# Differential attention: the score products of the two maps issued in turns, behind one wait for both exponentials

## The chip, the cores and the metric

The kernel runs on 1 core of a Trainium2 chip. The metric is the time of one execution in device microseconds (us). The kernel before takes 4272.95 us (median of 3 runs, 4268.02 to 4278.03).

## The reference

One step of a two-layer backbone for 512 latent tokens and 128 context tokens. The change lies in layer 0, which mixes tokens by differential attention with 8 heads. Each head has two score maps c = 0, 1, each from 64 rows of query and key:

```
s = einsum('bqhd,bkhd->bhqk', qblk, k) * scale      # q, k: 2 * 8 maps of width 64
p = softmax(s)                                      # per map
w = p[:, :, 0] - lam * p[:, :, 1]                   # one weight map per head
o = einsum('bhqk,bkhd->bqhd', w, v)                 # v: width 128 per head
```

Latent queries read 512 latent keys and 128 cached context keys in one softmax. The 128 context queries read only their own 128 keys. After the attention come a norm, an output product, and PEER expert retrieval; layer 1 uses another attention (MLA) and PEER again.

## The kernel before

The program is a row of blocks, with a barrier of all engines at the end of each: modulation and norms, q/k/v products (`diff_qkv`), `diff_attention` (lines 439 to 569), a norm (`diff_subnorm`), the output product (`out_product`), the experts, then the same for layer 1. The change touches only `scores(w)` in `diff_attention`.

`diff_attention` works through 40 items, 8 heads times 5 query blocks of 128 queries. Blocks 0 to 3 of a head are latent (640 keys), block 4 is context (128 keys). The order of each engine is written out by hand, and the engines are tied by semaphores:

- TensorE (PE), in iteration w: the scores of item w (lines 455 to 465), the product with V of item w-3 (`values`, line 484), the transposes of item w-2 (`turns`, line 474). The scores of map c go to PSUM banks 2c and 2c+1: 512 columns in the first, 128 in the second (lines 461, 462), or 128 columns alone for a context item (line 464). The operands are float32, and each such product appears in the trace as two weight loads (PEld) and two matmuls. Map 0 reads partitions 0 to 63 of q and k, map 1 partitions 64 to 127.
- VectorE (DVE): `maxima(w+1)`, then `weights(w)`. `maxima` waits for the scores of map 0 (`da_s` at 2w+1), takes the row maximum (line 515) and scales it (517), then does the same for map 1 (`da_s` at 2w+2). `weights` turns the two exponentials into one weight map (523 to 529).
- ScalarE (ACT): the two exponentials of item w (`exps`, line 547), each behind its scaled maximum; then the copy of the transposes of item w-2 (556) and of the result of item w-3 (561).

There is one set of score banks. So the scores of map c of item w wait until the exponential of the same map of item w-1 has read its banks: `da_exp` at 2(w-1)+c+1 in line 459. The semaphore goes up once per exponential, at the end of its ACTIVATION_READ_ACCUMULATOR.

Of the kernel before, what the change touches and what calls it, by code (L numbers as in the profile page):

```python
# [25 lines left out]
P = 128  # L26
D = 1024
DC = D // P
TS, TP, TC = 512, 128, 128
T = TS + TP  # L30
TK = T + TC
# [28 lines left out]
def mixed(nc, cst, inp, outs, g_dram, x_dram):  # L60
# [3 lines left out]
    def sem(name):  # L64
        if name not in sems:
            sems[name] = es.enter_context(nc.semaphore(name))
        return sems[name]

    def sb(stack, name, shape, dt=F32):
        return stack.enter_context(nc.sbuf_tensor(name, shape, dt))  # L70
# [18 lines left out]
    ps = es.enter_context(nc.psum_tensor("ps", [P, 8, 512], F32))  # L89
# [3 lines left out]
    def bank2(b, n=T, p=P):  # L93

        return ps[0:p, b:b + 2, :].rearrange("p a n -> p (a n)")[:, 0:n]
# [343 lines left out]
    def diff_attention(qT, kT, V, rsq, oT, pr, pT):  # L439

        items = [(hd, qb) for hd in range(HDA) for qb in range(TB)]

        def width(qb):
            return T if qb < 4 else TP

        with nc.Block() as block:
            @block.sync
            def _(sp):
                sp.wait_ge(sem("stored"), 32)

            @block.tensor
            def _(pe):
                def scores(w):
                    hd, qb = items[w]
                    for c in range(2):
                        q = qT[64 * c:64 * c + 64, hd, qb * P:(qb + 1) * P]
                        k = kT[64 * c:64 * c + 64, hd, :]
                        if w:
                            pe.wait_ge(sem("da_exp"), 2 * (w - 1) + c + 1)
                        if qb < 4:  # L460
                            pe.matmul(ps[:, 2 * c, :], q, k[:, 0:TS], start=True, stop=True)
                            mm = pe.matmul(ps[:, 2 * c + 1, 0:TC], q, k[:, T:TK], start=True, stop=True)
                        else:
                            mm = pe.matmul(ps[:, 2 * c, 0:TP], q, k[:, TS:T], start=True, stop=True)
                        mm.then_inc(sem("da_s"), 1)

                def turns(w):
                    hd, qb = items[w]
                    blocks = (0, 1, 2, 3, 5) if qb < 4 else (4,)
                    pe.wait_ge(sem("da_w"), 8 * (w + 1) + (4 if w + 1 < len(items) else 0))  # L470
                    if w >= 1:
                        pe.wait_ge(sem("da_pT"), w)
                    for k in range(len(blocks)):
                        mm = pe.transpose(bank2(4)[:, k * P:(k + 1) * P], pr[:, w % 3, 0, k * P:(k + 1) * P], ident)
                    mm.then_inc(sem("da_t"), 1)

                def values(w):
                    hd, qb = items[w]
                    blocks = (0, 1, 2, 3, 5) if qb < 4 else (4,)
                    pe.wait_ge(sem("da_pT"), w + 1)  # L480
                    if w >= 2:
                        pe.wait_ge(sem("da_o"), w - 1)
                    for k, kb in enumerate(blocks):
                        mm = pe.matmul(ps[:, 6 + w % 2, 0:P], V[:, kb, hd * P:(hd + 1) * P], pT[:, w % 2, k * P:(k + 1) * P],
                                       start=k == 0, stop=k == len(blocks) - 1)
                    mm.then_inc(sem("da_pv"), 1)

                for w in range(len(items) + 3):
                    if w < len(items):
                        scores(w)  # L490
                    if w >= 3:
                        values(w - 3)
                    if 2 <= w < len(items) + 2:
                        turns(w - 2)

            @block.vector
            def _(v):
                s = sem("da_w")
                M = len(items)

                def z_(w):
                    return small[:, 16 * (w % 2):16 * (w % 2) + 16]

                def at(w, k):

                    if k <= 4:
                        return k if w == 0 else 8 * w - 4 + k
                    return 8 * w + k + (4 if w + 1 < M else 0)

                def maxima(w):  # L510
                    hd, qb = items[w]
                    n, z = width(qb), z_(w)
                    for c in range(2):
                        v.wait_ge(sem("da_s"), 2 * w + c + 1)
                        v.tensor_reduce(z[:, c:c + 1], bank2(2 * c, n), AX, ALU.max).then_inc(s, 1)
                        v.wait_ge(s, at(w, 2 * c + 1))
                        v.tensor_scalar(z[:, 2 + c:3 + c], z[:, c:c + 1], rsq[:, 1, qb, 2 * hd + c:2 * hd + c + 1],
                                        None, ALU.mult).then_inc(s, 1)

                def weights(w):  # L520
                    n, z = width(items[w][1]), z_(w)
                    v.wait_ge(sem("da_exp"), 2 * w + 2)
                    v.reciprocal(z[:, 6:8], z[:, 4:6]).then_inc(s, 1)
                    v.wait_ge(s, at(w, 5))
                    v.tensor_tensor(z[:, 8:9], z[:, 7:8], lam[:, 4:5], ALU.mult).then_inc(s, 1)
                    p0, p1 = pr[:, w % 3, 0, 0:n], pr[:, w % 3, 1, 0:n]
                    v.tensor_scalar(p0, p0, z[:, 6:7], None, ALU.mult).then_inc(s, 1)
                    v.wait_ge(s, at(w, 7))
                    v.scalar_tensor_tensor(p0, p1, z[:, 8:9], p0, ALU.mult, ALU.add).then_inc(s, 1)

                maxima(0)
                for w in range(M):
                    if w + 1 < M:
                        maxima(w + 1)
                    weights(w)

            @block.scalar
            def _(act):
                def exps(w):
                    hd, qb = items[w]  # L540
                    n = width(qb)
                    z = small[:, 16 * (w % 2):16 * (w % 2) + 16]
                    if w >= 3:
                        act.wait_ge(sem("da_t"), w - 2)
                    for c in range(2):
                        act.wait_ge(sem("da_w"), 2 * c + 2 if w == 0 else 8 * w - 2 + 2 * c)
                        act.activation(pr[:, w % 3, c, 0:n], bank2(2 * c, n), ACT.Exp, bias=z[:, 2 + c:3 + c],
                                       scale=rsq[:, 2, qb, 2 * hd + c:2 * hd + c + 1], accum_out=z[:, 4 + c:5 + c]).then_inc(sem("da_exp"), 1)

                def copies(w):  # L550
                    hd, qb = items[w]
                    n = width(qb)
                    act.wait_ge(sem("da_t"), w + 1)
                    if w >= 2:
                        act.wait_ge(sem("da_pv"), w - 1)
                    act.copy(pT[:, w % 2, 0:n], bank2(4, n)).then_inc(sem("da_pT"), 1)

                def results(w):
                    hd, qb = items[w]
                    act.wait_ge(sem("da_pv"), w + 1)  # L560
                    act.copy(oT[:, hd, qb * P:(qb + 1) * P], ps[:, 6 + w % 2, 0:P]).then_inc(sem("da_o"), 1)

                for w in range(len(items) + 3):
                    if w < len(items):
                        exps(w)
                    if 2 <= w < len(items) + 2:
                        copies(w - 2)
                    if w >= 3:
                        results(w - 3)
# [1083 lines left out]
    with es:  # L1653
        with ExitStack() as st:
# [3 lines left out]
            kT = sb(st, "kT", [P, HDA, TK])  # L1658
            norm(0, 0, kT[:, :, 0:T])
            qT = sb(st, "qT", [P, HDA, T])  # L1660
# [9 lines left out]
        with ExitStack() as st:  # L1670
# [19 lines left out]
            qT, kT = sb(st, "qTm", [P, GH, T]), sb(st, "kTm", [P, GH, TK])  # L1690
# [157 lines left out]
```

## Time and profile before

| | |
|---|---|
| profiled execution, its own time | 4264.01 us |
| its span | 4262.2 us |
| span of `diff_attention` in it | about 381.1 to 535.2 us |
| PE busy in the whole span | 3871.4 us (91%) |
| DVE busy | 3205.7 us (75%) |
| ACT busy | 1703.4 us (40%) |
| mean granted TensorE clock | 0.959 |

Times in the trace are counted from the start of the span. The granted clock is a share of 2.4 GHz: 1.00 is 2.4 GHz and 0.50 is 1.2 GHz. PEld is the weight load, which can lie beside PE's matmuls. An engine that issues its instructions in order and waits for a semaphore is idle; "idle before <-releaser" names what ended the idle time.

### The profile page before, as it was taken

How to read it: one execution, taken by the hardware profiler on the slowest of the kernel's cores; microseconds unless marked ns; L12 is line 12 of the kernel's file. 1: busy time of each engine (PE TensorE's matmuls, PEld its weight loads, DVE VectorE, ACT ScalarE, POOL GpSimd, SP SyncE). 2: the span in 40 equal slices, each digit the busy share in tenths (PEclk: the TensorE clock that was granted, in tenths of full speed). 3: DMA queues.
4: the chain of work that ended last, by engine and by line, in shares of the span. 5: the costliest groups of instructions: out<-in, count | busy, mean ns of one | idle time of the engine just before them, and what ended most of it. 6: DMA issues, size and time to landing. Idle time of an engine off the chain costs nothing. (4 is left out here: it accounts for less than half of the span.)

```text
span 4262.2 us, 54821 instructions
## 1 busy us (share of the span) xinstructions
PE 3871.4 (91%) x20309; PEld 3151.3 (74%) x20309; DVE 3205.7 (75%) x6654; ACT 1703.4 (40%) x2834; POOL 985.9 (23%) x788
## 2 busy tenths in 40 slices
PE   4999998958799999999988988989479999999998
PEld 1554647846699999999964565669379999999997
DVE  2563815684699999999971443339979999999997
ACT  1112602235544444444432454322474444444443
POOL 0000000024433333333310000000363333333331
PEclk8999989978899999999999999999799999999999
DMA  4320013217899999999951000120299999999996
GB/s 191 144 89 30 1 40 128 90 50 198 284 421 416 408 403 402 408 406 406 401 222 70 20 20 20 36 82 2 69 290 421 418 405 405 409 405 401 405 407 276
DMA packets 267689, 1033.64 MB, mean 243 GB/s; under 512 B 147008, under 2 KB 150016, under 8 KB 159360
## 3 DMA queue, kind: packets, MB, share of 16 engines
q0 software_dynamic: 76032, 553.68, 32.3%
q1 hardware_dynamic: 191392, 476.46, 29.4%
q8 instruction: 162, 2.65, 0.3%
q14 instruction: 103, 0.84, 0.1%
HBM read 970.69 MB, written 59.39 MB: 242 GB/s over the span
## 5 line engine op out<-in xcount | busy, mean ns | idle before, releaser
L1430 POOL DMA_INDIRECT gbuf<-in_uv,rows x340 | 517.7, 1523 | 876.9 <-DVE hT L1597 807.1
L1225 POOL TENSOR_SCALAR pqT<-iota,selT 128x128 f32<-128x128 f32 x256 | 202.2, 804 | 1621.7 <-ACT selT L1171 1503.5
L1597 DVE SCALAR_TENSOR_TENSOR hT<-gbuf,act,hT 128x1024 f32<-128x1024 f32 x336 | 416.9, 1282 | 6.0
L1582 DVE SCALAR_TENSOR_TENSOR gbuf<-gbuf,ht 128x1024 f32<-128x1024 f32 x340 | 402.1, 1220 | 5.0 <-DMA gbuf<-in_uv,rows 5.0
L100 PE MATMUL ps<-hT,ring 128*128 128x512 f32 (+1 forms) x624 | 325.5, 604 | 47.9 <-DMA ring<-in_wts 32.4
L1430 POOL DMA_INDIRECT xT<-in_uv,rows x172 | 257.2, 1495 | 469.4 <-DVE hT L1597 394.5
L1444 PE MATMUL ps<-h1h,U1h 128*128 128x384 f32 x1024 | 344.9, 337 | 9.8 <-DVE U1l L1556 9.8
L1444 PE MATMUL ps<-h0h,U0h 128*128 128x384 f32 x1024 | 345.1, 337 | 8.9 <-DVE U0l L1556 8.9
L1444 PE MATMUL ps<-h0h,U0l 128*128 128x384 f32 x1024 | 344.7, 337 | 0.0
L1444 PE MATMUL ps<-h1h,U1l 128*128 128x384 f32 x1024 | 344.5, 336 | 0.0
L1444 PE MATMUL ps<-h0l,U0h 128*128 128x384 f32 x1024 | 344.4, 336 | 0.0
L1444 PE MATMUL ps<-h1l,U1h 128*128 128x384 f32 x1024 | 344.1, 336 | 0.0
L1508 ACT ACTIVATE ring<-ps 128x384 f32<-128x384 f32 x256 | 125.9, 492 | 424.8 <-PE ps L1444 424.3
L1110 PE MATMUL ps<-pqT,w 128*128 128x128 f32 x1536 | 205.2, 297 | 71.3 <-DVE w L1358 39.6
L1110 PEld LDWEIGHTS ps<-pqT,w 128*128 128x128 f32 x1536 | 196.8, 211 | 83.8 <-issue 65.7
L1061 PE MATMUL ps<-hT,ring 128*128 128x128 f32 x1920 | 223.3, 278 | 27.2 <-PEq L210 27.2
L1061 PEld LDWEIGHTS ps<-hT,ring 128*128 128x128 f32 x1920 | 219.8, 194 | 31.5 <-issue 31.5
L101 PEld LDWEIGHTS ps<-hT,ring 128*128 128x128 f32 (+1 forms) x624 | 118.9, 191 | 153.8 <-issue 153.8
L1518 ACT ACTIVATE act<-act 128x2 f32<-128x2 f32 x256 | 52.2, 204 | 417.5 <-DVE gbuf L1582 284.6
L1582 DVE SCALAR_TENSOR_TENSOR xT<-xT,ht 128x1024 f32<-128x1024 f32 x172 | 203.6, 1220 | 12.7 <-DMA xT<-in_uv,rows 12.7
L1597 DVE SCALAR_TENSOR_TENSOR hT<-xT,act,hT 128x1024 f32<-128x1024 f32 x168 | 208.4, 1282 | 3.0
L1444 PEld LDWEIGHTS ps<-h1h,U1h 128*128 128x128 f32 x1024 | 193.6, 189 | 13.2 <-DVE U1l L1556 6.5
(346 smaller groups left out, 8867.5 us busy)
## 6 DMA issues: line engine op xcount, KB each, us to landing
ring<-in_u SPq DMA_DIRECT2D x128, 1024.0 KB, 12.0
ring<-in_v SPq DMA_DIRECT2D x128, 1024.0 KB
ring<-in_wts SPq DMA_DIRECT2D x26, 2048.0 KB, 8.3
gates<-ring SPq DMA_DIRECT2D x32, 1536.0 KB, 7.8
ring<-gates SPq DMA_DIRECT2D x64, 768.0 KB, 16.0
xT<-in_ada_late SPq DMA_DIRECT2D x24, 1024.0 KB, 5.1
abuf<-in_ada_mid POOLq DMA_DIRECT2D x16, 1024.0 KB, 5.2
gbuf<-in_uv,rows POOLq DMA_INDIRECT x340
```

The source lines that it names most:

```text
L100: e.matmul(out[:, 0:512], lhsT, rhs[:, 0:512], start=start, stop=stop)
L101: return e.matmul(out[:, 512:n], lhsT, rhs[:, 512:n], start=start, stop=stop)
L1061: mm = pe.matmul(ps[:, 5 + n % 3, q * P:(q + 1) * P], w[:, dc, q * P:(q + 1) * P], hT[:, dc, tb * P:(tb + 1) * P], start=dc == 0, stop=dc ...
L1110: mm = pe.matmul(ps[:, b + t // 4, (t % 4) * P:(t % 4 + 1) * P], one1[:, r % 2, t, :], one2[:, r % 2, t, :], start=True, stop=True)
L1225: last = pool.tensor_scalar(one2[:, r % 2, t, :], iota[:], selT[:, 1, t0 + t:t0 + t + 1], selT[:, 2, t0 + t:t0 + t + 1], ALU.is_equal, ALU ...
L1430: pool.indirect_dma_start(out=slots[m % GSLOTS], out_offset=None, in_=inp[f"uv{l}"], in_offset=bass.IndirectOffsetOnAxis(ap=rows[:, c:c + ...
L1444: mm = pe.matmul(up_bank(k), Us[x][:, k, dc * P:(dc + 1) * P], hs[y][:, dc, :], start=dc == 0 and x + y == 0, stop=dc == DC - 1 and x == 1)
L1508: act.activation(Wf[:, k, :], up_bank(k), ACT.Gelu_apprx_tanh).then_inc(sem(n_ + "gelu"), 1)
L1518: act.activation(act4[:, n % 2, 0:2], act4[:, n % 2, 0:2], ACT.Gelu_apprx_tanh)\
L1582: v.scalar_tensor_tensor(u, u, 1.0, ht[:, m // P, :], ALU.mult, ALU.mult, accum_out=act4[:, n % 2, m % 2:m % 2 + 1]).then_inc(sem(n_ + "do ...
L1597: v.scalar_tensor_tensor(y, x, w, y, ALU.mult, ALU.add).then_inc(sem(n_ + "acc"), 1)
```

## The change

`scores(w)` now has one wait, for both exponentials of item w-1 (`da_exp` at 2w), ahead of everything. Then the products are issued map by map in turns: 512 columns of map 0, 512 of map 1, 128 of map 0, 128 of map 1; for a context item 128 of map 0, 128 of map 1. The last product of each map raises `da_s` as before. Banks, operands, sizes and the number of instructions are the same, but for one wait fewer per item. VectorE and ScalarE are untouched.

```diff
 def scores(w):
     hd, qb = items[w]
-    for c in range(2):
-        q = qT[64 * c:64 * c + 64, hd, qb * P:(qb + 1) * P]
-        k = kT[64 * c:64 * c + 64, hd, :]
-        if w:
-            pe.wait_ge(sem("da_exp"), 2 * (w - 1) + c + 1)
-        if qb < 4:
-            pe.matmul(ps[:, 2 * c, :], q, k[:, 0:TS], start=True, stop=True)
-            mm = pe.matmul(ps[:, 2 * c + 1, 0:TC], q, k[:, T:TK], start=True, stop=True)
-        else:
-            mm = pe.matmul(ps[:, 2 * c, 0:TP], q, k[:, TS:T], start=True, stop=True)
-        mm.then_inc(sem("da_s"), 1)
+    if w:
+        pe.wait_ge(sem("da_exp"), 2 * w)
+    pieces = ((0, 0, TS), (1, T, TK)) if qb < 4 else ((0, TS, T),)
+    for part, a, b in pieces:
+        for c in range(2):
+            mm = pe.matmul(ps[:, 2 * c + part, 0:b - a], qT[64 * c:64 * c + 64, hd, qb * P:(qb + 1) * P],
+                           kT[64 * c:64 * c + 64, hd, a:b], start=True, stop=True)
+            if part == len(pieces) - 1:
+                mm.then_inc(sem("da_s"), 1)
```

## Rows read from the trace of the kernel before

**Rows 1.** The page's chain that ended last, shares of the span by engine.

```profile
PE 24%; DVE 1%; DMA 0%; issue 0%; POOL 0%; ACT 0%; ACTq 0%; DVEq 0%; POOLq 0%
```

**Rows 2.** Waits, 381:535: who waited for whom: us in total, times, longest.

```profile
ACT pr_da L547 <- DVE small L517: 47.1, 39, 2.7
...
PEld ps L461 <- ACT pr_da L547: 19.5, 48, 2.4
DVE small L515 <- PE ps L462: 17.8, 18, 3.4
PE ps L461 <- ACT pr_da L547: 8.8, 16, 2.1
```

**Rows 3.** Timeline, 430:447: a latent item (start us, length us, engine, line).

```profile
431.78 0.88 ACT L547 ACTIVATE pr_da<-ps,small,rsq 128x640 f32<-128x640 f32 x1 [1.40 <-DVE small L517]
...
432.70 0.89 ACT L547 ACTIVATE pr_da<-ps,small,rsq 128x640 f32<-128x640 f32 x1
...
432.81 1.61 PE L461 MATMUL ps<-kT,qT 64*128 64x512 f32 x3 [0.38 <-ACT pr_da L547]
...
433.43 0.88 DVE L529 SCALAR_TENSOR_TENSOR pr_da<-pr_da,small 128x640 f32<-128x640 f32 x1
...
433.73 0.18 PEld L461 LDWEIGHTS ps<-kT,qT 64*128 64x128 f32 x1 [0.20 <-ACT pr_da L547]
433.77 0.38 PE L462 MATMUL ps<-kT,qT 64*128 64x128 f32 x2
...
434.23 0.82 DVE L515 TENSOR_REDUCE small<-ps 128x1 f32<-128x640 f32 x1
...
435.00 1.38 PE L484 MATMUL ps<-pT_da,V 128*128 128x128 f32 x10
...
435.39 0.88 ACT L547 ACTIVATE pr_da<-ps,small,rsq 128x640 f32<-128x640 f32 x1 [0.97 <-DVE small L517]
...
436.22 0.71 PE L474 MATMUL ps<-consts,pr_da 128*128 128x128 f32 x5
...
436.31 0.89 ACT L547 ACTIVATE pr_da<-ps,small,rsq 128x640 f32<-128x640 f32 x1
```

**Rows 4.** The same timeline: the context item behind it, then the next head.

```profile
436.86 0.96 PE L464 MATMUL ps<-kT,qT 64*128 64x128 f32 x4
...
437.34 0.29 PEld L464 LDWEIGHTS ps<-kT,qT 64*128 64x128 f32 x2 [0.18 <-ACT pr_da L547]
...
437.85 0.28 DVE L515 TENSOR_REDUCE small<-ps 128x1 f32<-128x128 f32 x1
...
439.78 1.15 PE L461 MATMUL ps<-kT,qT 64*128 64x512 f32 x4
...
440.74 0.41 PE L462 MATMUL ps<-kT,qT 64*128 64x128 f32 x4
...
441.08 1.38 PE L484 MATMUL ps<-pT_da,V 128*128 128x128 f32 x10
441.16 0.82 DVE L515 TENSOR_REDUCE small<-ps 128x1 f32<-128x640 f32 x1 [0.69 <-PE ps L462]
...
443.25 0.88 ACT L547 ACTIVATE pr_da<-ps,small,rsq 128x640 f32<-128x640 f32 x1
```

**Rows 5.** Windows: stretch, length, busy of PE, PEld, DVE, ACT, POOL, granted clock, DMA.

```profile
381.00:401.00 20.00, 16.55 (x50) 10.38 (x51) 12.67 (x28) 9.60 (x18) 0.00 (x0) 0.52 0.09 27
421.00:441.00 20.00, 19.16 (x118) 13.50 (x116) 17.34 (x45) 13.58 (x36) 0.00 (x0) 1.00 0.00 1
1030.20:1033.60 3.40, 1.30 (x7) 0.34 (x4) 1.03 (x1) 2.06 (x8) 0.85 (x2) 1.00 1.14 267
1033.60:1037.00 3.40, 3.08 (x14) 3.11 (x15) 0.00 (x0) 3.15 (x8) 0.00 (x0) 0.50 0.75 270
```

**Rows 6.** Timeline of PE, 385:388.5: map 0 of the second item.

```profile
385.34 2.20 PE L461 MATMUL ps<-kT,qT 64*128 64x512 f32 x3 [2.09 <-ACT pr_da L547]
```

**Rows 7.** Timeline of DVE, 385:390: the maximum behind it.

```profile
387.88 0.82 DVE L515 TENSOR_REDUCE small<-ps 128x1 f32<-128x640 f32 x1 [2.62 <-PE ps L462]
```

## The prediction

> **What bounds the kernel now.** I read the chain of waits first. PE holds 24% of the span there [rows 1], but nearly all of that is the expert layers, which the change does not touch. The question is only how long `diff_attention` takes. It lasts from 381.1 to 535.2 us and ends in a barrier, it moves next to no data (DMA share 0.00 in its middle [rows 5]), and nothing of the next block can start earlier. So I take each microsecond that it gains or loses to arrive whole at the end.
>
> Inside it PE looks like the bound: it is busy 19.16 of 20 us, DVE 17.34, ACT 13.58 [rows 5]. That reading is false, as the waits show. ACT waited 39 times for the scaled maximum, 47.1 us in all. PE and its weight loads waited 19.5 + 8.8 us, 64 times, for an exponential before a 512-column score product [rows 2]. What turns is a loop with one set of score banks: exponential, score products into the freed banks, maximum, exponential.
>
> The timeline of a latent item gives its length [rows 3]. The exponential of map 0 starts at 431.78, PE starts map 0 of the next item at 432.81 (1.03 later), DVE starts its maximum at 434.23 (1.42 later), ACT starts the next exponential of map 0 at 435.39 (1.16 later). Sum 3.61 us. Map 1 runs through the same loop 0.92 us behind: exponential 432.70, products from 433.73, exponential 436.31. Two other things fit closely into this loop. DVE finishes the weights at 433.43 + 0.88 = 434.31, just when it begins the maximum, so it has no idle time here either. And PE needs 435.00 - 432.81 = 2.19 us for the scores with their stagger, 1.22 for the values, 0.64 for the transposes.
>
> **The change part by part.**
>
> *The order of the products.* It aims at running the two maps beside each other in the array, since one uses the upper and the other the lower 64 rows. The trace already shows this in the kernel before, wherever both banks are free in time. After a context item all four matmuls of line 461 lie in 1.15 us from 439.78, the four of line 462 in 0.41 us from 440.74, and the values start at 441.08: 1.30 us for both maps [rows 4]. One map by itself needs about as long: map 0 from 432.81 to the end of its 128 columns at 433.77 + 0.38 = 434.15, 1.34 us [rows 3]. Even in the staggered item the first load of map 1 (433.73) comes before map 0's 128-column products (433.77). So the old order does not hold map 1 back; only its wait does. I cost the new order at nothing. Bounds: it cannot beat the 1.30 us by more than some hundredths, since one map alone takes 1.34; at worst the alternation works less well and a pair takes the staggered 2.19 us, 0.9 more per item.
>
> The Trainium skill, page "TensorE: Matmul & The Clock Gate", section "Step-by-step: what each phase is for", says that matmuls stay in program order and only weight loads are pulled ahead. By that, the old order would keep map 1 behind all of map 0 and the new order alone would open the overlap. The rows above disagree for map 1's matmuls, which start with map 0's [rows 4]. The same skill's page "TensorEngine Tiling (Array Packing)", section "Key Properties", says that different tiles can execute in parallel, and there the trace agrees, 1.15 us for four matmuls.
>
> *The wait.* Map 0 now waits for the exponential of map 1 too. In a latent item behind a latent one that moves its start from 432.81 to 433.73, by 0.92 us. Map 1 starts at 433.73 as before and ends as before. What PE has queued behind, values at 435.00 and transposes at 436.22, follows map 1 and does not move in this item. What moves is DVE: the maximum of map 0 was taken while PE worked on map 1. Now both maps come together at 433.73 + 1.38 = 435.11 (1.38 is 439.78 to 441.16 [rows 4]) and DVE takes them one after the other. DVE has nothing to put in the gap: the weights of the item before are done at 434.31.
>
> The new loop, from the exponential of map 1 to the next one: 1.03 us to the products (432.70 to 433.73 [rows 3]), 1.38 to the first maximum, 2.09 to the exponential of map 1 (441.16 to 443.25 [rows 4]). Sum 4.50 us against 3.61: **+0.89 us**. The first such step of a head starts from two maps that run together, so it pays the whole stagger of 0.92. PE then has 1.30 + 1.22 + 0.64 = 3.16 us of work in 4.50, DVE its 3.6 [rows 3], so neither takes over.
>
> *Which items pay.* Each head has five steps.
> - Into latent blocks 1, 2 and 3, behind a latent item: 0.92 + 0.89 + 0.89 = 2.70 us.
> - Into the context block: map 0 started at 436.86 because PE was still at the transposes, map 1 at 437.34, and DVE came to it at 437.85, just free of the weights. From the exponential at 436.31 that is 1.54. After the change: 1.03 of wait, 0.48 of products (437.34 to 436.86 + 0.96 = 437.82), 0.03 to DVE, again 1.54. Cost 0.
> - Into block 0 behind the context item: both exponentials are short and done, both maps start together at 439.78 already [rows 4]. Cost 0.
>
> So 2.70 us a head, 8 heads: **+21.6 us**.
>
> *The start.* From 381 to 401 us the clock is 0.52 [rows 5], and three of the first head's steps fall there. A map takes 387.88 - 385.34 = 2.54 us instead of 1.38 [rows 6, 7]. The added stagger there is one exponential with its mean and read, about 0.98, so nearly the same price. Where the clock rises in the new kernel no row tells. If it rises at the same time, the slower loop has done one item less at 1.2 GHz and saves about 1.2; some microseconds later, it gives that back. I take -0.6 and hold +/-1.5. Sum: +21.0 us.
>
> On the profiled execution that makes 4264.0 + 21.0 = 4285.0 us. The median of the runs stands 8.9 us above that execution, so **4294 us** for the median.
>
> **The rivals.**
>
> *A. The clock falls in the pauses.* The new loop leaves PE idle for 4.50 - 3.16 = 1.3 us per latent item, and for 2.0 to 2.3 us where the values belong to a context item (1.22 becomes some 0.3). For: elsewhere PE was busy 1.30 of 3.40 us, and the clock was 0.50 right behind [rows 5]. Near the context item of each head it will be about as little busy for as long. The pattern repeats in each head, so it may hit all heads or none. Against: the stage keeps 1.00 once warm [rows 5], and most of the new loop is busier than that. Price: at 1.2 GHz a map takes 2.54 instead of 1.38, 1.2 us per item and loop. With one or two items per head, +1.2 to +2.4, over 7 heads +8 to +17: 4302 to 4311, say 4306. If the clock stayed low in the whole stage, 32 latent items with 1.2 to 1.6 each would add 38 to 50: about 4338.
>
> *B. Faster: PE is the bound after all.* If PE's order is what closes the loop, the alternation takes 2.19 - 1.30 = 0.89 us from each of 32 latent items: -28 us, 4245. It decides from the point where PE comes to the scores after the exponential of map 1 has ended. PE's 96% busy speaks for it, and the context item, where PE is late by some 0.5 us. Against it: PE waits for the exponential 64 times [rows 2], and in rows 3 it reaches map 0 before the exponential of map 1 is done. The skill's program-order rule quoted above would lead to this case too, if the old order serialised the maps more often than rows 4 shows.
>
> *C. No change: the late map 0 is covered.* If DVE, not the loop of banks, set the pace, a later map 0 would meet a DVE that is still at the weights. DVE is full, for it. But its weights end 0.08 us after map 0 is ready (434.31 against 434.23 [rows 3]), so 0.8 of the 0.92 stays uncovered. Time 4273 to 4280.
>
> *D. The new order serialises more.* A pair takes up to 2.19 instead of 1.30: up to 24 x 0.89 = 21 us more, 4315. Nothing in the trace speaks for it.
>
> **How the numbers follow.** Forecast 55%, A 28% (of it 4 with the clock low throughout), B 4%, C 7%, D 6%. The time is the forecast's, 4294 us. Its own spread is +/-7: 5 for the runs (4268 to 4278 before), the rest for the start and the positions of the clock. The range leaves out B, most of C, the low clock throughout and the worst of D: 4282 to 4313. A difference under 0.2% (8.5 us) is what a measurement can't tell from none. Faster by more than that: B, 0.04. Within it: C, 0.07. Slower: forecast, A and D, 0.89.
>
> **What would show it.** Right, if in the changed profile the maximum of map 0 (line 515) starts every 4.5 us in latent items behind latent ones, if PE's first score products start 1.03 us after the start of the exponential of map 1, if both maps' products lie in 1.3 us, and if the stage ends near 556 us instead of 535. A clock under 1.00 between 405 us and the stage's end shows A. A loop of 3.6 us shows C, a shorter one B, a pair of over 1.5 us at clock 1.00 D. I am wrong in kind if DVE's wait for PE before line 515, 17.8 us before [rows 2], does not grow by about 20 us.

## The result and the profile after

The changed kernel takes 4293.23 us (median of 5 runs, 4290.36 to 4297.24), against 4274.95 for the kernel before (5 runs beside it). The ratio is 1.0045, 95% interval 1.0031 to 1.0060: slower by 18 us. The forecast was 4294, which was 4272.95 for the kernel before plus 21.0; two more runs of that kernel moved its median up by 2.0, and the change cost 18.3.

The profiled execution of the changed kernel has a span of 4288.6 us, 26.4 more than the one of before. Of these, 21.0 arise in `diff_attention`: from the first maximum to the last result it lasts 172.80 us instead of 151.77. The forecast for the stage was +21.0. The other 5 us lie outside it, in stages the change does not touch. A kernel with a stage 1.5 us shorter than before showed 15 us more outside the stage in its one profile (span 4275.3), so a single span is no measure of a few microseconds; the length of the stage is.

The timeline of the changed kernel at clock 1.00, a latent item behind a latent one (start us, length us, engine, line; the maximum is now line 513, the exponential 545, all score products 460, values 482). These rows answer to [rows 3]:

```profile
457.55 0.88 ACT L545 ACTIVATE pr_da<-ps,small,rsq 128x640 f32<-128x640 f32 x1 [2.28 <-DVE small L515]
...
458.47 0.88 ACT L545 ACTIVATE pr_da<-ps,small,rsq 128x640 f32<-128x640 f32 x1
...
459.20 0.88 DVE L527 SCALAR_TENSOR_TENSOR pr_da<-pr_da,small 128x640 f32<-128x640 f32 x1
...
459.50 1.35 PE L460 MATMUL ps<-kT,qT 64*128 64x512 f32 x8 [2.18 <-ACT pr_da L545]
...
460.78 1.38 PE L482 MATMUL ps<-pT_da,V 128*128 128x128 f32 x10
460.88 0.82 DVE L513 TENSOR_REDUCE small<-ps 128x1 f32<-128x640 f32 x1 [0.80 <-PE ps L460]
...
461.87 0.82 DVE L513 TENSOR_REDUCE small<-ps 128x1 f32<-128x640 f32 x1
...
462.05 0.89 ACT L545 ACTIVATE pr_da<-ps,small,rsq 128x640 f32<-128x640 f32 x1 [1.86 <-DVE small L515]
...
462.97 0.88 ACT L545 ACTIVATE pr_da<-ps,small,rsq 128x640 f32<-128x640 f32 x1
```

From the exponential of map 1 (458.47) to the products is 1.03 us, to the first maximum 1.38, to the next exponential of map 1 (462.97) 2.09: 4.50 us, each term as forecast. All eight matmuls of both maps lie in 1.35 us from 459.50. PE was idle 2.18 us before them, DVE 0.80 us before the maximum, where it had no gap before [rows 3].

The waits of the changed kernel, 381:558 (us in total, times, longest), answer to [rows 2]:

```profile
ACT pr_da L545 <- DVE small L515: 69.1, 39, 3.7
PEld ps L460 <- ACT pr_da L545: 60.1, 33, 3.4
PE ps L460 <- ACT pr_da L545: 52.1, 31, 3.1
DVE small L513 <- PE ps L460: 38.7, 32, 3.6
```

ACT waits 22 us longer for the maxima (69.1 for 47.1) and DVE 21 us longer for PE (38.7 for 17.8). The last is the row that the prediction named as its test in kind. PE and its loads stood 28.3 us before an exponential's end in the kernel before (19.5 + 8.8); now the loads alone stand 60.1 us.

The windows of the changed kernel (length, busy PE, PEld, DVE, ACT, POOL, granted clock) answer to [rows 5]:

```profile
417.80:421.20 3.40, 3.40 (x19) 2.69 (x15) 2.09 (x6) 1.04 (x4) 0.00 (x0) 0.50 0.00 0
...
438.30:441.70 3.40, 3.40 (x14) 2.17 (x13) 1.61 (x4) 0.59 (x3) 0.00 (x0) 0.50 0.00 0
461.00:481.00 20.00, 13.43 (x98) 9.88 (x98) 15.76 (x40) 11.99 (x30) 0.00 (x0) 1.00 0.00 1
```

PE is busy 13.4 of 20 us where it was 19.2. Twice the clock falls to 0.50 for 3.4 us, in heads 1 and 2, which the kernel before did not show once its clock had risen. Both falls come right behind a pause of PE of 2.18 us (414.94 to 417.12 and 435.88 to 438.06). Later heads have the same pause and keep 1.00.

### The profile page after: what moved, and what is told of

Its sections match the earlier page's. It is cut to its first block and busy times, and to the rows that moved or that the text cites. A ratio compares the mean times of both kernels' runs of the same rounds, so it can differ in the third digit from the quotient of the medians.

```text
span 4288.6 us, 54821 instructions
## 1 busy us (share of the span) xinstructions
PE 3852.1 (90%) x20309; PEld 3141.7 (73%) x20309; DVE 3206.1 (75%) x6654; ACT 1703.8 (40%) x2834; POOL 987.9 (23%) x788
## 5 line engine op out<-in xcount | busy, mean ns | idle before, releaser
L100 PE MATMUL ps<-hT,ring 128*128 128x512 f32 (+1 forms) x624 | 325.5, 604 | 47.1 <-DMA ring<-in_wts 31.6
```

Of the source, the lines that this page charges most:

```text
L100: e.matmul(out[:, 0:512], lhsT, rhs[:, 0:512], start=start, stop=stop)
```

## The experiments

The stage is always taken from the first maximum to the last result, from one profile per kernel; the times are medians with the ratio to the kernel before on the same chip. A step is the time from the first maximum of one item to that of the next, and a step "into block 2" ends at query block 2. A head is called warm if the clock had risen before it began.

| kernel | step, latent behind latent, clock 1.00 | stage us | time us | ratio (95%) |
|---|---|---|---|---|
| before | 3.58 to 3.62 | 151.77 | 4274.95 | |
| the change | 4.50 | 172.80 | 4293.23 | 1.0045 (1.0031 to 1.0060) |
| wait only | 4.50 | 173.46 | 4295.26 | 1.0053 (1.0036 to 1.0071) |
| order only | 4.29 | 166.45 | 4292.66 | 1.0045 (1.0028 to 1.0062) |
| joint wait in the free steps | 3.58 to 3.62 | 150.30 | 4277.14, one run | |
| joint wait in one step | 4.50 in that one | 164.38 | 4279.62, one run | |
| wait before the tail | 3.64 | 152.31 | 4274.46 | 1.0002 (0.9992 to 1.0011) |
| filler products | 4.50 | 171.35 | 4292.12, one run | |
| two sets of banks, first form | 5.5 into blocks 1 and 3, about 4.2 into block 2 | 197.40 | 4317.24 | 1.0109 (1.0092 to 1.0125) |
| first form, wait for the item ahead | 5.5, 6.3 and 6.8 in most heads | 221.95 | 4339.80 | 1.0150 (1.0133 to 1.0167) |
| two sets, scores issued early | 3.25 to 3.28 | 130.15 | 4245.54 | 0.9934 (0.9921 to 0.9947) |
| the same, wait for the item ahead | 5.88 and more | 260.15 | 4387.47 | 1.0274 (1.0251 to 1.0297) |

### Only the wait

```diff
 hd, qb = items[w]
+if w:
+    pe.wait_ge(sem("da_exp"), 2 * w)
 for c in range(2):
     ...
-    if w:
-        pe.wait_ge(sem("da_exp"), 2 * (w - 1) + c + 1)
```

> The old order of the products, with the one wait for both exponentials ahead of them. Theory (the wait is the whole cost, and the array runs the two maps side by side in either order): latent items behind latent ones every 4.50 us as in the changed kernel, against 3.61 before; the stage from the first maximum to the last result 172 to 173 us against 151.8 before and 172.8 in the changed kernel; 19 to 23 us slower than before in all. Rival 1 (part of the loss is the new order): the loop comes out under 4.4 us, the gain of it under 18 us. Rival 2 (matmuls run in program order, so the old order serialises the maps): the loop is still 4.50, because VectorE comes to map 1 only 0.99 us after map 0, but the values start 2.2 us after the first score product and not 1.3.

Measured: steps of 4.50 us, stage 173.46, ratio 1.0053. Its timeline (maximum L515, products L461 and L462, values L484, exponential L547), two items at clock 1.00:

```profile
461.23 1.19 PEld L484 LDWEIGHTS ps<-pT_da,V 128*128 128x128 f32 x10
...
461.32 0.82 DVE L515 TENSOR_REDUCE small<-ps 128x1 f32<-128x640 f32 x1 [0.80 <-PE ps L462]
...
466.88 1.14 PE L461 MATMUL ps<-kT,qT 64*128 64x512 f32 x4
...
467.84 0.39 PE L462 MATMUL ps<-kT,qT 64*128 64x128 f32 x4
...
468.17 1.38 PE L484 MATMUL ps<-pT_da,V 128*128 128x128 f32 x10
```

The four 512-column matmuls lie in 1.14 us and the values come 1.29 us after the first product, not 2.2. So the old order runs the maps side by side too, as in [rows 4], and with the joint wait the order makes no difference to the step. The joint wait alone is enough for the whole loss. Its clock, once risen, fell twice as well, at 414.8 and at 517.2.

### Only the order

```diff
-if w:
-    pe.wait_ge(sem("da_exp"), 2 * w)
 for part, a, b in pieces:
     for c in range(2):
+        if w and part == 0:
+            pe.wait_ge(sem("da_exp"), 2 * (w - 1) + c + 1)
         mm = pe.matmul(ps[:, 2 * c + part, 0:b - a], ...
```

> The new order of the products with a wait of its own for each map, placed at that map's 512-column product: 512 of map 0, wait, 512 of map 1, 128 of map 0, 128 of map 1. Theory (the other map's products do not hold back a product of another row group, only the wait ahead of it does): map 0's 128 columns start just behind the wait for map 1's exponential, about where they started before (433.77 against a wait that ends at 433.73), so the loop stays at 3.6 to 3.75 us and the time within 4 us of before. Rival (matmuls run in program order): map 0's 128 columns come behind the 0.85 us of map 1's 512, its maximum 0.8 us later, the loop is 4.3 to 4.5 us and the time 17 to 21 us slower.

My theory fell here. The step is 4.29 us and the stage 166.45, so the new order without the joint wait costs 0.68 us a step. (The clock fell twice in this stage, at 498.6 and 519.1; 4.29 is the step at clock 1.00.) Taking the joint wait out of the changed kernel therefore wins back only 0.21 us of the 0.89: either part of the change is enough for most of the loss. The timeline of that kernel (L460 products, L513 maximum):

```profile
456.47 0.29 PEld L460 LDWEIGHTS ps<-kT,qT 64*128 64x128 f32 x2 [1.31 <-ACT pr_da L545]
456.47 2.26 PE L460 MATMUL ps<-kT,qT 64*128 64x512 f32 x8 [1.07 <-ACT pr_da L545]
...
457.39 0.30 PEld L460 LDWEIGHTS ps<-kT,qT 64*128 64x128 f32 x4 [0.62 <-ACT pr_da L545]
...
457.92 0.19 PEld L460 LDWEIGHTS ps<-kT,qT 64*128 64x128 f32 x1 [0.23 <-issue]
458.35 0.19 PEld L460 LDWEIGHTS ps<-kT,qT 64*128 64x128 f32 x1 [0.24 <-issue]
458.56 0.82 DVE L513 TENSOR_REDUCE small<-ps 128x1 f32<-128x640 f32 x1 [0.59 <-PE ps L460]
```

From 457.39 four loads lie in 0.30 us: two for map 1's 512 columns and two for map 0's last 128, its tail. So the products of map 0's tail are recorded beside those of map 1; taken singly, the last matmul of the tail is recorded from 457.61 to 457.88. But DVE, idle for 0.59 us, begins its maximum only at 458.56. The last matmul that stands ahead of the tail in the program, the second of map 1's 512 columns, is recorded to 458.51. PE alone, 457.9 to 458.34, shows these two matmuls of map 1 and no longer the tail (457.39 + 1.12 = 458.51):

```profile
457.39 1.12 PE L460 MATMUL ps<-kT,qT 64*128 64x512 f32 x2
```

A theory for this: two row groups (the 64 rows of each map) run side by side, but their matmuls finish, and raise semaphores, in the order of the program. The next experiment tests it.

### The wait before the tail

```diff
     pe.matmul(ps[:, 2 * c, :], q, k[:, 0:TS], start=True, stop=True)
+    if w and c == 0:
+        pe.wait_ge(sem("da_exp"), 2 * w)
     mm = pe.matmul(ps[:, 2 * c + 1, 0:TC], q, k[:, T:TK], start=True, stop=True)
```

> The kernel before, with the wait for map 1's exponential placed one product earlier: 512 columns of map 0, wait for both, 128 of map 0, then 512 and 128 of map 1. Against the kernel with the new order and a wait per map (loop 4.29 us) only the place of map 0's 128 columns differs: ahead of map 1's 512 in the program instead of behind. Theory (products of the two row groups start side by side, but they finish, and raise their semaphore, in the order of the program; in that kernel map 0's 128 columns ended at 457.88 and VectorE began only at 458.56, behind the end of map 1's 512 at 458.51): here nothing of map 1 stands ahead, so map 0 is reported 0.45 us behind the wait, at the time of before: loop 3.6 to 3.7 us, stage 151 to 155 us, time within 4 us of before. Rival (the wait ahead of the 128 columns is what costs in that kernel): loop 4.2 to 4.3 us, stage about 168 us, 15 us slower.

Measured: steps of 3.64 us, stage 152.31, ratio 1.0002. Its timeline (L461 512 columns, L464 128 columns, L517 maximum):

```profile
446.56 1.62 PE L461 MATMUL ps<-kT,qT 64*128 64x512 f32 x3
...
447.48 0.18 PEld L464 LDWEIGHTS ps<-kT,qT 64*128 64x128 f32 x1 [0.62 <-ACT pr_da L549]
447.48 0.18 PEld L461 LDWEIGHTS ps<-kT,qT 64*128 64x128 f32 x1
447.52 0.44 PE L464 MATMUL ps<-kT,qT 64*128 64x128 f32 x2
...
448.00 0.83 DVE L517 TENSOR_REDUCE small<-ps 128x1 f32<-128x640 f32 x1
448.02 0.59 PE L461 MATMUL ps<-kT,qT 64*128 64x512 f32 x1
```

Here map 0's tail and map 1's first load start together at 447.48, as they did in the order-only kernel. DVE begins at 448.00, 0.04 us after the tail's end (447.96), before the second matmul of map 1's 512 columns has even started (448.02). The tail waits for the same semaphore value in both kernels; only what stands ahead of it in the program differs. So the wait ahead of the tail costs 0.03 us a step, and the tail's place behind map 1's 512 columns the other 0.65. That its semaphore comes behind them is shown. Whether the array really worked on the tail as early as recorded, or only its report was late, is not: the ends in a profile are modelled.

The Trainium skill, page "TensorE: Matmul & The Clock Gate", section "The mechanism" of its part on packing small matmuls, says that matmuls keep the order of the program in their starts and their ends. The ends agree with these two kernels: behind the start of map 1's loads the maximum comes 458.56 - 457.39 = 1.17 us later with the tail last, and 448.00 - 447.48 = 0.52 us later with the tail first. The recorded starts do not: the first matmul of map 1 is recorded from 433.73, with its load, and map 0's tail, which stands before it in the program, from 433.77 [rows 3].

### The steps that should be free, and one that should pay

The joint wait in the old order, for some query blocks only:

```diff
-    pe.wait_ge(sem("da_exp"), 2 * (w - 1) + c + 1)
+    pe.wait_ge(sem("da_exp"), 2 * w if qb in (0, 4) else 2 * (w - 1) + c + 1)
```

> The old order; the joint wait only for query blocks 0 and 4 of each head, the steps that the prediction costs at nothing. Theory: stage 151.8 us as before, within 0.5. Rival (each joint wait costs some of the stagger, also there): 0.3 to 0.9 us for each of 15 steps, 156 to 165 us.

Measured: stage 150.30 us; the steps into block 4 take 3.63 and those into block 0 3.30, against 3.61 and 3.32 before. The stage is shorter because the clock rose at 395.2 us, 17.0 us after it fell at 378.2; in the kernel before it took 20.5 (381.6 to 402.1). So these 15 waits cost nothing, as forecast, within 0.02 us each.

With `qb == 2` in place of `qb in (0, 4)`:

> The old order; the joint wait only for query block 2 of each head, one of the three steps that the prediction lets pay. Theory: that step becomes 4.5 us instead of 3.6, 8 times, the steps beside it stay: stage 151.8 + 7.2 = 159.0 us (the first at the lower clock pays 0.98). Rival (the delay is made up in the next step, where PE and VectorE have room): 152 to 155 us.

The step into block 2 is 4.50 us in each of the seven warm heads, and in heads with the clock at 1.00 the next ones are 3.62, 3.61 and 3.32: nothing is made up. But the stage is 164.38, 5.4 us over the 159.0 expected. The step into block 4 was 6.05, 4.78, 6.05 and 4.75 us in four heads, and the clock was 0.50 there (from 414.8, 455.8, 493.3 and 534.3). One of these stretches:

```profile
414.80:421.60 6.80, 6.75 (x27) 4.86 (x26) 4.38 (x10) 3.36 (x8) 0.00 (x0) 0.50 0.01 2
```

The excess of these four steps over 3.61 is 2.44 + 1.17 + 2.44 + 1.14 = 7.2 us; the first head (20.88 us), warm sooner, gives 2.6 of it back. So the fall of the clock that rival A of the prediction feared showed itself here, with a single delayed step per head. The kernel with the order alone, whose pauses of PE are 1.1 us, had two falls as well, so which pause is followed by a fall is not settled by these profiles.

### Filler products in the pauses

```diff
     turns(w - 2)
+if 4 <= w < len(items) and w % TB < 4:
+    pe.wait_ge(sem("da_o"), w - 3)
+    for _ in range(2 if w % TB == 2 else 1):
+        pe.matmul(ps[:, 6 + w % 2, P:4 * P], ident, consts[:, 0:3, :]..., start=True, stop=True)
```

> The changed kernel with one extra float32 product of 384 columns (two for query block 2) behind the transposes of each latent item, into free columns of a result bank; its result is not read. It fills PE's pauses of 1.3 us (2.0 to 2.3) with about 0.65 us (1.3). Theory (the two dips of the granted clock in the changed kernel's stage, at 417.8 and 438.3, come from the pauses): no dip behind the start of the stage, each head 20.4 us. The stage then loses the 0.5 + 1.0 us of the two dips. Rival (dips come from elsewhere, or the extra products delay the scores): dips remain, or the loop is over 4.6 us.

Measured: no fall of the clock between 402.2 us and 555.8, where the stage is over, heads of 20.42 to 20.66 us, stage 171.35 against 172.80. Windows:

```profile
421.00:441.00 20.00, 16.65 (x108) 11.21 (x107) 15.48 (x40) 11.99 (x30) 0.00 (x0) 1.00 0.00 1
441.00:461.00 20.00, 16.65 (x107) 11.14 (x107) 15.40 (x41) 12.00 (x30) 0.00 (x0) 1.00 0.00 1
```

The 1.45 us regained are the price of the two falls (steps of 4.99 and 5.46 instead of 4.50). It is one profile each; the falls also differ between the change (two) and the wait-only kernel (at 414.8 and 517.2), which have the same loop. That the pauses allow them is likely from these kernels, but one profile of the filler does not show that it prevents them. In the time of the kernel 1.5 us cannot be told.

### Two sets of score banks

If the cost of the joint wait is that there is one set of banks, a second set must take it off the path. The kernel's eight banks do not hold two sets of four with transposes and results, so both maps share a middle bank (in outline):

```diff
+def maps(w, n):                       # [P, 2, n]: map c at 512 * 3 * (w % 2) + 896 * c
+    at = 3 * 512 * (w % 2)
+    return ps...[:, at:at + 1792].rearrange("p (c n) -> p c n", c=2)[:, :, 0:n]
 # scores(w), latent:
+if w >= 2:
+    pe.wait_ge(sem("da_exp"), 2 * (w - 1))
+# map 1: keys 0..127 to the middle bank; map 0: 512; map 1: 384 + 128 to its own bank;
+# wait for the first of these; map 0: its last 128 to the middle bank
 # maxima(w):
+v.wait_ge(sem("da_s"), 2 * w + 2)
+v.tensor_reduce(z[:, 0:2], maps(w, n), AX, ALU.max)
+v.tensor_tensor(z[:, 2:4], z[:, 0:2], rsq[:, 1, qb, 2 * hd:2 * hd + 2], ALU.mult)
 # turns(w), before the fifth transpose (it shares the last bank with the results):
+if k == 4 and w >= 1:
+    pe.wait_ge(sem("da_o"), w)
 # ScalarE: exps(w), results(w - 3), copies(w - 2)
```

> Two sets of score banks of three banks each: scores of item w wait for both exponentials of item w-2. For it map 1's first 128 columns lie in the bank of map 0's last 128, so both maps come ready together, one maximum instruction takes both maps, one multiplication scales both, and the exponentials wait for both; transposes and results share the last two banks and the result is copied ahead of the transposes. Theory (the joint wait costs because there is one set of banks; with two it is off the path, and VectorE's own work sets the pace: 1.5 for the maximum of 1280 columns, 0.2 for the scale, 1.75 for the weights): a latent item every 3.4 to 3.6 us, stage 140 to 150 us, 2 to 12 us faster than before. Rival (what costs is that the maps come together, so that maxima and exponentials follow each other and nothing overlaps): 4.5 us or more per item, stage over 170.

A miss: 1.0109, latent steps of 5.5 us into blocks 1 and 3 and about 4.2 into block 2. The waits say why, and that it is neither the theory nor its rival (L484 transposes, L569 the copy of a result), 384:582:

```profile
PEld ps L484 <- ACT hT L569: 55.3, 27, 3.3
DVE small L524 <- PE ps L468: 51.3, 24, 3.5
PE ps L484 <- ACT hT L569: 48.8, 22, 3.1
```

I had made a new wait. The fifth transpose waits for the copy of a result, which ScalarE makes only after both exponentials of the item, and the next item's scores stood behind that transpose in PE's queue. PE's pauses came with falls of the clock, too: its mean in this stage is 0.85, against 0.94 before; how much of the loss is the clock's was not separated.

> The kernel with two sets of score banks, but with the wait of the change: scores of item w wait for both exponentials of item w-1. Only that wait differs from the kernel with two sets. Theory: the wait closes the loop again: 1.03 to the products, 1.4 to the maximum, 1.8 through the maximum of both maps and its scale to the first exponential, 0.92 to the second: 5.1 to 5.2 us per latent item, stage 185 to 192 us, 35 to 45 us slower than with two sets and no such wait. Rival (the wait is harmless once banks are free): as with two sets alone.

The one line changed here, `da_exp` at 2w, costs 1.0150 against 1.0109, some 22 us where 35 to 45 were expected. Both forms are bound by the new loop, and the mean clock of the stage is 0.78 in the second and 0.85 in the first, so the pair does not price the wait.

The second form moves the scores out of that queue:

```diff
+scores(0)
 for w in range(len(items) + 3):
-    if w < len(items):
-        scores(w)
+    if w + 1 < len(items):
+        scores(w + 1)
```

> The kernel with two sets of score banks and joint waits, with the scores of item w+1 issued ahead of the values of item w-3 and the transposes of item w-2. In the first form of it the scores stood behind the fifth transpose, which waits for the copy of a result that ScalarE makes only after both exponentials, and the loop was 5.5 us. Theory (the bank wait and that order were the loops; VectorE's own 3.3 us per latent item are left: 464.61 to 467.94 in that form): a latent item every 3.3 to 3.5 us, stage 138 to 148 us, 4 to 14 us faster than before, though both maps still wait for both exponentials of an item. Rival (that maps come and are taken together keeps the loop long): over 4 us.

Measured: 4245.54 us, 0.9934 (0.9921 to 0.9947), 28 us faster than the kernel before and 48 faster than the change. The latent steps are 3.25 to 3.28 us, the step into block 0 2.27, the stage 130.15. VectorE's part of its timeline (L525 maximum of both maps, L527 scale, L538 end of the weights), and ScalarE's exponentials:

```profile
448.62 1.49 DVE L525 TENSOR_REDUCE small<-ps 128x2 f32<-128x1280 f32 x1
...
450.14 0.16 DVE L527 TENSOR_TENSOR small<-small,rsq 128x2 f32<-128x2 f32 x1
...
450.40 0.89 ACT L556 ACTIVATE pr_da<-ps,small,rsq 128x640 f32<-128x640 f32 x1
...
451.07 0.88 DVE L538 SCALAR_TENSOR_TENSOR pr_da<-pr_da,small 128x640 f32<-128x640 f32 x1
...
451.28 0.88 ACT L556 ACTIVATE pr_da<-ps,small,rsq 128x640 f32<-128x640 f32 x1
...
451.87 1.48 DVE L525 TENSOR_REDUCE small<-ps 128x2 f32<-128x1280 f32 x1
```

The next maximum (451.87) starts when the weights of the item before end (451.07 + 0.88): in this step VectorE has no idle time, and its maximum waits for no scores. (Into block 1 it is idle for 0.7 us a head, and there PE has no pause.) Both maps still wait for both exponentials of an item, come together, and are taken together, as in the change. One instruction for both maps takes 1.49 us where two took 0.82 each, and one scale 0.16 where there were two of 0.21 with a wait each: that is how 3.61 became 3.26. So the second set took the wait off the path, but the gain over the kernel before in this step is the shorter work of VectorE. There VectorE had no gap in the steps into blocks 2 and 3 either (434.23 in [rows 3]); only into block 1 did it wait:

```profile
427.00 0.82 DVE L515 TENSOR_REDUCE small<-ps 128x1 f32<-128x640 f32 x1 [0.68 <-PE ps L462]
```

No kernel has two sets of banks and two separate maxima, so how the 28 us divide between the second set and the merged maximum is not shown.

The counter-test puts the wait of the change back in and leaves all else:

> The fast form with two sets of score banks, with one line changed: scores of item w wait for both exponentials of item w-1, as in the change, and not of item w-2. Everything else, the maximum of both maps in one instruction too, is as in the fast form. Theory (the joint wait for the item just ahead is what closes the loop): 0.88 from the first to the second exponential, 1.03 to the products, 1.35 to the maximum, 1.78 through it and the scale to the next first exponential: 5.0 to 5.1 us per latent item behind a latent one instead of 3.3, stage about 40 us longer than in the fast form. Rival (the gain of the fast form is the merged maximum and not the second set): the loop stays under 4 us.

Measured: 1.0274, stage 260.15 us, twice as long. The direction is that of the theory and excludes its rival, but the size is three times what I expected. In the stage the mean granted clock is 0.74:

```profile
384.00:640.00 256.00, 161.39 (x833) 131.10 (x833) 114.06 (x240) 96.25 (x236) 0.00 (x0) 0.74 0.00 1
```

The shortest latent steps at clock 1.00 are 5.88 us, not 5.05. With the scores ahead of the values and transposes in PE's queue, the copies that ScalarE makes before the next exponentials come later too (L565 the copy of the transposes):

```profile
445.60 0.16 DVE L527 TENSOR_TENSOR small<-small,rsq 128x2 f32<-128x2 f32 x1
```

```profile
446.02 0.69 ACT L565 COPY pT_da<-ps 128x640 f32<-128x640 f32 x1 [0.42 <-PE ps L484]
446.61 0.89 ACT L556 ACTIVATE pr_da<-ps,small,rsq 128x640 f32<-128x640 f32 x1
```

The scaled maximum is done at 445.76, and the exponential starts 0.85 us later, behind that copy. The rest goes with the clock: the latent steps that touch stretches at 0.50 take 6.1 to 8.0. How the two parts divide was not separated.

## Why the prediction was right

Time, stage and direction came out as forecast, and most steps held one by one. Two terms of the sum did not, and that their errors cancelled was luck. So was the last microsecond of the time: the median of the kernel before stood 2.0 us higher with more runs, and the difference of the medians is 2.7 us under the 21.0.

- *The loop of banks bounds the stage, not PE.* Held. PE's busy time fell from 19.2 to 13.4 of 20 us, while the stage grew. The kernel with a second set of banks, early scores and one maximum for both maps made it 21.6 us shorter. VectorE's own work was nearly as long as the loop, as the prediction says ("DVE its 3.6"), so a second set by itself would probably have had little to win in the steps into blocks 2 and 3.
- *Map 0 moves by the stagger: +0.92, +0.89, +0.89 a head.* Held: 4.50 us in every latent step at clock 1.00, and in heads 3, 4, 5 20.43 us against 17.75, +2.68 where 2.70 was forecast.
- *The steps into blocks 4 and 0 cost nothing.* Held, in the changed kernel (3.64 and 3.30) and alone.
- *The new order costs nothing.* True only beside the joint wait, since both maps then end within 0.01 us of each other. By itself the order costs 0.68 us a step, because map 0's tail is reported behind map 1's 512 columns. This is the term that the prediction put at nothing. The two parts of the change are not additive: 0.89 for the wait, 0.68 for the order, 0.89 for both. The sentence that "the old order does not hold map 1 back; only its wait does" is right, but I did not see that the new order holds map 0 back.
- *The start: -0.6 against the other heads, so +2.1.* Mis-sized. The first head took 23.25 us against 22.48, only +0.8: the clock rose after 13.6 us for one stretch and for good after 20.5, with fewer items at half speed by then.
- *The clock keeps 1.00 (the forecast), or falls once a head for 8 to 17 us (rival A).* Between the two: it fell in two heads and cost 0.5 and 1.0 us. These 1.5 us hide the 1.3 that the first head came out short.

Rivals B and C are excluded for the change by the step of 4.50 us and by DVE's gap of 0.80 us before the maximum; D by the pair in 1.35 us. The 0.08 us of cover that C reads from 434.31 against 434.23 is no cover: 434.23 is the start of the maximum, and map 0's products were recorded as ended at 434.15. The 18.3 us between the medians are less than the 21.0 of the stage; the interval, 13 to 26 us, holds both.

## What to carry to other kernels

Where two streams share a pipeline with one set of buffers, their stagger is work in parallel: a joint wait makes both as late as the later one, and costs the stagger in each round. Look whether the array already overlaps the two (loads of both within some ns, the follower 1.3 us behind) before reordering to obtain it. If the two are issued in turns behind waits of their own, the first is reported as late as the other's products that stand ahead of its last one: 0.68 us a step here. To take a wait off the path, add a buffer set and then check what stands behind each new wait in the queue, and which engine is as busy as the loop was long: here the same kernel, with VectorE's two maxima made one in both forms, was 1.1% slower with the scores behind a waiting transpose and 0.7% faster with them ahead.

## What the runs showed of the hardware that I had not expected

- Matmuls of different row groups are recorded as started out of program order (map 1 at 433.73, map 0's tail at 433.77 [rows 3]), but a semaphore of one came only when those ahead in the program had ended: 458.56 behind an end at 458.51, though its own end is recorded at 457.88.
- With the joint wait in one step per head, the granted clock fell from 1.00 to 0.50 in four of eight heads, for 3.4 or 6.8 us, at 1.1 to 2.4 us each. The kernel before, with 0.9 us less of PE's pause in that step, kept 1.00. These are one profile each, and that the pause is the cause is not shown.
- The maximum over 1280 columns in two maps took 1.49 us against 2 x 0.82, and the scale of both 0.16 against 2 x 0.21.
